# Two-layer decoder trunk, one core: ScalarE copies both halves of the transposed attention probabilities, and the end norm is applied to token rows

## The reference, cut to what matters

```python
# sliding window attention: 16 query heads of 64, 128-token blocks, window of 2 blocks
logits = jnp.concatenate([scores, sink], axis=-1)
m = jnp.max(logits, axis=-1, keepdims=True)
p = jnp.exp(logits - m)
probs = p[..., :-1] / jnp.sum(p, axis=-1, keepdims=True)
out = jnp.einsum('bkgnij,bnjkd->bnikgd', probs.astype(v.dtype), v2)
...
# after the two layers
y = x * lax.rsqrt(jnp.mean(x * x, axis=-1, keepdims=True) + NORM_EPS)
return y * final_norm
```

## Time and profile before

| | |
|---|---|
| median of 3 runs | 2602.13 us |
| the profiled execution, own time | 2599.23 us |
| its span, first to last instruction | 2597.4 us |
| TensorE busy | 2502.4 us (96%) |
| VectorE busy | 1537.0 us (59%) |
| ScalarE busy | 869.8 us (33%) |
| the two stretches with the head groups | 500 to 740 us, 1766 to 1996 us |
| from the last unit to the end | 2577.5 to 2597.4 us |

### The profile page before, as it was taken

One profiled execution on the slowest core, in us unless ns is written; L12 is line 12 of the kernel. 1 busy time (PEld: TensorE's weight loads), 2 busy tenths in 40 slices (PEclk: granted clock), 3 DMA queues, 4 the chain that ended last, 5 costly groups with the idle time before them and its releaser, 6 DMA issues.

```text
span 2597.4 us, 35934 instructions
## 1 busy us (share of the span) xinstructions
PE 2502.4 (96%) x11581; PEld 2045.3 (79%) x11581; DVE 1537.0 (59%) x2345; ACT 869.8 (33%) x1320; POOL 212.9 (8%) x167
## 2 busy tenths in 40 slices
PE   5999999999999999999999999999999999999998
PEld 4788888777678878888878888887777888788886
DVE  6876778566644467633477767866665445633333
ACT  2331233545422243222332222344543223331222
POOL 5100003000000040000030000210000002200001
PEclk7999999999999999999999999999999999999999
DMA  6465664311123425523336656532111343233332
GB/s 222 125 199 166 194 183 132 122 56 50 57 68 96 129 88 170 159 85 96 110 91 194 188 177 195 160 122 60 54 57 49 99 128 97 85 100 95 95 111 66
DMA packets 494952, 307.19 MB, mean 118 GB/s; under 512 B 8904, under 2 KB 488472, under 8 KB 494232
## 3 DMA queue, kind: packets, MB, share of 16 engines
q1 hardware_dynamic: 427288, 239.10, 31.1%
q10 hardware_dynamic: 67584, 67.12, 8.1%
HBM read 299.89 MB, written 6.29 MB: 118 GB/s over the span
## 4 chain that ended last, share of the span: by engine, by line
PE 76%; DVE 13%; ACT 5%; issue 4%; POOL 1%; DVEq 0%; DMA 0%; ACTq 0%; SPq 0%; POOLq 0%
PE ps_proj L1468 23%; PE ps_proj L1469 23%; PE ps_proj L1470 23%; ACT sb_scratch L680 2%; DVE sb_w_lo L871 2%; DVE sb_small L1142 2%; DVE sb_scratch L1139 1%; PE ps_mid L1624 1%; PE ps_mid L1626 1%; PE ps_mid L1625 1%; DVE sb_scratch L1162 1%; PE ps_mid L1672 1%; POOL sb_scratch L461 1%; DVE sb_h_lo L938 1%; DVE sb_scratch L883 1%
## 5 line engine op out<-in xcount | busy, mean ns | idle before, releaser
L1468 PE MATMUL ps_proj<-sb_a_hi,sb_w_hi 128*128 128x512 f32 x1888 | 736.1, 390 | 3.0 <-DVE sb_w_lo L871 3.0
L1470 PE MATMUL ps_proj<-sb_a_hi,sb_w_lo 128*128 128x512 f32 x1888 | 734.7, 389 | 0.0
L1469 PE MATMUL ps_proj<-sb_a_lo,sb_w_hi 128*128 128x512 f32 x1888 | 734.5, 389 | 0.0
L533 ACT ACTIVATE sb_w_hi<-sb_raw 128x1024 fp32r<-128x1024 f32 (+1 forms) x388 | 431.0, 1111 | 872.6 <-PE ps_proj L1470 833.2
L871 DVE TENSOR_TENSOR sb_w_lo<-sb_raw,sb_w_hi 128x1024 fp32r<-128x1024 f32 (+1 forms) x388 | 503.4, 1297 | 310.9 <-ACT sb_w_hi L533 295.5
L1468 PE MATMUL ps_proj<-sb_h_hi,sb_w_hi 128*128 128x512 f32 x1280 | 511.9, 400 | 10.7 <-DVE sb_w_lo L871 6.3
L1469 PE MATMUL ps_proj<-sb_h_lo,sb_w_hi 128*128 128x512 f32 x1280 | 502.7, 393 | 0.0
L1470 PE MATMUL ps_proj<-sb_h_hi,sb_w_lo 128*128 128x512 f32 x1280 | 502.2, 392 | 0.0
L1468 PEld LDWEIGHTS ps_proj<-sb_a_hi,sb_w_hi 128*128 128x128 f32 x1888 | 354.4, 188 | 79.4 <-issue 3.0
L1470 PEld LDWEIGHTS ps_proj<-sb_a_hi,sb_w_lo 128*128 128x128 f32 x1888 | 354.4, 188 | 73.3
L1469 PEld LDWEIGHTS ps_proj<-sb_a_lo,sb_w_hi 128*128 128x128 f32 x1888 | 354.4, 188 | 73.0
(11 more groups left out here) (162 smaller groups left out, 1863.4 us busy)
## 6 DMA issues: line engine op xcount, KB each, us to landing
sb_raw<-in_ffn_w_up SPq DMA_DIRECT2D x176, 512.0 KB, 3.8
sb_scratch<-in_w_ada ACTq DMA_DIRECT2D x128, 512.0 KB, 4.2
sb_raw<-in_w_in SPq DMA_DIRECT2D x100, 512.0 KB, 3.8
sb_raw<-in_ffn_w_down SPq DMA_DIRECT2D x64, 704.0 KB, 4.5
sb_raw<-in_w_branch_swa SPq DMA_DIRECT2D x16, 512.0 KB, 3.6
sb_raw<-in_w_branch_ret SPq DMA_DIRECT2D x16, 512.0 KB, 3.6
sb_raw<-in_w_out SPq DMA_DIRECT2D x16, 512.0 KB, 3.6
sb_scratch<-in_w_ada SPq DMA_DIRECT2D x14, 512.0 KB, 7.4
```

The lines of the kernel that those rows point to most:

```text
L533: act.activation(Whi[s][:, 0:n], raw[s][:, 0:n], ACT.Copy).then_inc(hi_ready, 1)
L1468: pe.matmul(bank, Whi[s][:, w], hi, start=first, stop=False)
L1469: pe.matmul(bank, Whi[s][:, w], lo, start=False, stop=False)
L1470: return pe.matmul(bank, Wlo[s][:, w], hi, start=False, stop=last)
```

## The change

Two edits that have nothing to do with each other.

**Probabilities.** TensorE signals once after all 8 transposes, ScalarE copies both banks to SBUF in one instruction over 1024 columns, VectorE's `probs_out` is gone, and `swa_values` waits for ScalarE alone.

**End norm.** The final gain is multiplied into x by ScalarE tile by tile while the last units still run (`final_scale`, only in the last layer), behind the squares of the same tile. TensorE transposes the scaled but not yet normalised tiles into all eight PSUM banks: tiles 0 to 3 right behind the last unit into `pM`, then the sums of squares, then tiles 4 to 7 into `last_banks`. The blocks of one bank now belong to the same 128 tokens, so `rstd` is a number per partition: VectorE (features 0 to 511) and ScalarE (512 to 1023) multiply by it as they copy out, in 4 instructions each. Spreading `rstd`, VectorE's 8 products and ScalarE's 8 copies are gone. SyncE stores four pieces, one for each 128 tokens.

```diff
@@ last_banks @@
+        last_banks = [pA[0], pA[1], pO, pS]
@@ SyncE @@
-            for h in range(2):
-
-                sp.wait_ge(o_tok, 4 * (h + 1))
-                sp.dma_start(out[0].rearrange("(t p) d -> p t d", p=P)[:, :, 512 * h:512 * (h + 1)],
-                             out_tok[:, :, 512 * h:512 * (h + 1)]).then_inc(stored, 16)
-            sp.wait_ge(stored, 32)
+            for n in range(TT):
+
+                sp.wait_ge(o_first, n + 1)
+                sp.wait_ge(o_last, n + 1)
+                sp.dma_start(out[0].rearrange("(t p) d -> p t d", p=P)[:, n, :], out_tok[:, n, :]).then_inc(stored, 16)
+            sp.wait_ge(stored, 16 * TT)
@@ ScalarE @@
+            def final_scale(k):
+
+                act.activation(XV[:, k, :], XV[:, k, :], ACT.Copy, scale=vcols[:, bass.ds(GAIN_COL["final"] + k, 1)]).then_inc(z_ready, 1)
...
                                 square(3 * l + (3 if f else 1), 2 * j + s, s, bank_free[s], g0 + HALF + j + 2)
                                 in_next_layer(act, l, f, lambda: scaled_hi(3 * l + (3 if f else 1), 2 * j + s))
+                                if f:
+                                    in_last_layer(act, l, lambda: final_scale(2 * j + s))
...
             def probs_out(no):
-                act.wait_ge(pt_ps, 2 * no + 1)
-                act.activation(probs_t[:, 0:T], pM[:, 2, :], ACT.Copy).then_inc(pt_act, 1)
+                act.wait_ge(pt_ps, no + 1)
+                act.activation(probs_t.rearrange("p (a t) -> p a t", a=2), pM[:, 2:4, :], ACT.Copy).then_inc(pt_act, 1)
...
-            for k in range(KT):
-                act.wait_ge(y_out, k + 1)
-                act.activation(out_tok[:, :, P * k:P * (k + 1)], pA[k % 2][:, :].rearrange("p (t c) -> p t c", c=P),
-                               ACT.Copy).then_inc(o_tok, 1)
+            act.wait_ge(rstd_ready, 4 * DEPTH + 1)
+            for n in range(TT):
+                act.wait_ge(y_last, n + 1)
+                act.activation(out_tok[:, n, T:2 * T], last_banks[n][:, :], ACT.Copy, scale=rstd[:, n:n + 1]).then_inc(o_last, 1)
@@ VectorE @@
-            def probs_out(no):
-                dve.wait_ge(pt_ps, 2 * no + 2)
-                dve.tensor_copy(probs_t[:, T:2 * T], pM[:, 3, :]).then_inc(pt_dve, 1)
...
                     retention_rope(1, rk)
-                    probs_out(h0)
                     maxima(h0 + 2, l, i, 1, 0, 0)
                     normalise(h0 + 2, 0)
                     retention_gate(0)
-                    probs_out(h0 + 1)
                     maxima(h0 + 3, l, i, 1, 1, 1)
...
                     swa_out(2 * n0, 2 * i)
-                    probs_out(h0 + 2)
...
-                    probs_out(h0 + 3)
...
-            dve.wait_ge(rb_ready, 4 * DEPTH + 1)
-            for k in range(KT):
-                if k >= 2:
-                    dve.wait_ge(y_out, k - 1)
-                g = vcols[:, GAIN_COL["final"] + k:GAIN_COL["final"] + k + 1]
-                dve.scalar_tensor_tensor(tbuf[k % 2], pO[:, :], g, XV[:, k, :], ALU.mult, ALU.mult).then_inc(t_ready, 1)
+            dve.wait_ge(rstd_ready, 4 * DEPTH + 1)
+            for n in range(TT):
+                dve.wait_ge(y_first, n + 1)
+                dve.tensor_scalar(out_tok[:, n, 0:T], pM[:, n, :], rstd[:, n:n + 1], None, ALU.mult).then_inc(o_first, 1)
@@ TensorE @@
                         last = pe.transpose(pM[:, 2 + a, P * n:P * (n + 1)], probs[w][:, T * a + P * n:T * a + P * (n + 1)], ident)
-                    last.then_inc(pt_ps, 1)
+                last.then_inc(pt_ps, 1)
...
                 pe.wait_ge(pt_act, no + 1)
-                pe.wait_ge(pt_dve, no + 1)
...
+            def turn(bank, n, k, first):
+
+                return pe.transpose(bank[:, P * (k - first):P * (k - first + 1)], XV[:, k, P * n:P * (n + 1)], ident)
+
+            half = KT // 2
+            for k in range(half):
+                pe.wait_ge(z_ready, k + 1)
+                for n in range(TT):
+                    last = turn(pM[:, n, :], n, k, 0)
+                    if k == half - 1:
+                        last.then_inc(y_first, 1)
             sum_squares(3 * DEPTH)
-            spread_rstd(4 * DEPTH, pO, 0).then_inc(rb_ready, 1)
-            for k in range(KT):
-                pe.wait_ge(t_ready, LAYER_SPLITS * DEPTH + k + 1)
-                if k >= 2:
-                    pe.wait_ge(o_tok, k - 1)
-                for t in range(TT):
-                    last = pe.transpose(pA[k % 2][:, P * t:P * (t + 1)], tbuf[k % 2][:, P * t:P * (t + 1)], ident)
-                last.then_inc(y_out, 1)
+            for s in range(2):
+                pe.wait_ge(bank_free[s], LAYER_GATED * DEPTH + 1)
+            for n in range(TT):
+                if n == TT - 1:
+
+                    pe.wait_ge(rstd_ready, 4 * DEPTH + 1)
+                for k in range(half, KT):
+                    pe.wait_ge(z_ready, k + 1)
+                    last = turn(last_banks[n], n, k, half)
+                last.then_inc(y_last, 1)
```

More of the change, by code:

```diff
@@ L224, in decoder @@
         scores, max_ready, exp_ready, p_ready = sem("scores"), sem("max_ready"), sem("exp_ready"), sem("p_ready")
-        pt_ps, pt_act, pt_dve, o_ps, o_hi, o_done = (sem(n) for n in ("pt_ps", "pt_act", "pt_dve", "o_ps", "o_hi", "o_done"))
+        pt_ps, pt_act, o_ps, o_hi, o_done = (sem(n) for n in ("pt_ps", "pt_act", "o_ps", "o_hi", "o_done"))
         st_ps, st_done, y_ps, ysq, ysum, y_free, var_ps = (sem(n) for n in ("st_ps", "st_done", "y_ps", "ysq", "ysum", "y_free", "var_ps"))
         mg_ready, mg_hi, mg_lo = sem("mg_ready"), sem("mg_hi"), sem("mg_lo")
-        y_out, o_tok, stored = sem("y_out"), sem("o_tok"), sem("stored")
+        z_ready, y_first, y_last, o_first, o_last, stored = (sem(n) for n in ("z_ready", "y_first", "y_last", "o_first", "o_last", "stored"))
         carrier = {"pool": sem("pool_carrier"), "dve": sem("dve_carrier")}
@@ L314, in in_next_layer, with in_last_layer @@
                     work()
+        def in_last_layer(eng, l, work):
+            with eng.If(l > DEPTH - 2):
+                work()
         def next_layer(l):
```

## The result

The changed kernel took 2585.43 us as the median of 4 runs (2583.16 to 2586.3); the kernel before 2601.85 beside it (4 runs, 2599.65 to 2603.2). The profiled execution took 2585.38, its span 2583.6.

The account below looks back on a forecast made before the run. TensorE, busy 96% of the span, was taken as the bound, so only its idle time and the end could be won: 7.6 + 5.9 = 13.5 us off 2602.1 gives 2588.6 us, range 2586 to 2593.

Parts of the forecast that it names:

- the short waits in the head groups: TensorE's waits for VectorE's copy and maxima in 8 head groups: 7.6 us to be won in all.
- Values of h0: Head groups: the 0.70 us wait for VectorE's copy goes, 0.10 returns at scores of h0+3; net 0.60 each.
- Retention scores: Head groups: earlier maxima of h0+3 close the 0.14 us gap ahead of these scores; 0.12 counted each.
- Values of h0+2: Head groups: earlier maxima let ScalarE's copy end before TensorE comes, so the 0.32 us wait goes in each.
- Last step of head group 3: Transposes to values, no unit between: the longer ScalarE copy makes 0.88 us idle 1.24, a loss of 0.36, twice.
- cross-check with the 10.7 us of the waits' view: Head groups: summing from TensorE's 10.7 us of waits for VectorE's copy gave a gain of 7.7 us.
- No new wait: Head groups: waits for ScalarE's copy, about 1.2 us, only in head group 3; maxima waits up some 1.5.
- The end: Behind the last product: first store 5.6 us sooner, four stores' data without a gap; 5.9 us won.
- stores that pay their fixed part one by one: Rival at the final stores: each pays its fixed 1.43 us again; 4.3 us less won, 2592.9, chance 0.08.
- the rate of `x_spill`: Rival at the final stores: 2048 KB take 8.7 us from issue to landing; 1.8 less won, 2590.4, chance 0.17.
- The clock at the end: TensorE's clock around the final transposes: no cost counted; a fall would cost some 1.8 us, chance 0.02.
- carry to the median by the constant 2.9: Whole kernel: the runs' median stood 2.9 us above the profiled execution; that difference was carried over to the forecast.

Follow-up runs that it names:

- before again: The kernel before, nothing altered, run and profiled once more: 2603.21 us (one run).
- before filled: The kernel before plus 3 or 10 unused products between a norm's sum and the spreading of its factor: median 2597.96 us, ratio 0.9981.
- end norm alone: The changed kernel with the edit of the probabilities undone, so only the end edit against the kernel before: median 2595.82 us, ratio 0.9969.

## Why the prediction missed

The mechanism was right in each part, and two terms of the sum were too small, by more than the range allowed. The failed step is the pricing of the short waits in the head groups: 7.6 foreseen, 11.2 measured.

- **Values of h0**, 8 x 0.60 foreseen: 0.55 to 0.64 in head groups 0 to 2, 0.82 and 0.84 in head group 3, 5.2 in all. Right, but for head group 3, where a pause of 0.28 us in `normalise` of the step before (703.23 to 703.51, between the reciprocal and line 1162) is gone from VectorE's stream as well. It is a part of this edit's gain: all four traces with the old copies have it in both layers (before, before again, before filled, end norm alone), and none of the ten others has, the one with the copy of h0+1 put back included. What in VectorE's stream makes it is open.
- **Retention scores**, 8 x 0.12: 0.35 to 0.39 each, 3.0 in all where 0.96 was foreseen. This is more than half of the miss of 3.6. This step of the prediction read the gap between a modelled end and a start as the whole wait, and even took off from it; the copy put back alone costs 0.38 where 0.12 shows.
- **Values of h0+2**, 8 x 0.32: 0.38 to 0.41 each, 2.4 in the six of head groups 0 to 2, by the same fault.
- **Last step of head group 3**, a loss of 0.36: 0.25 by the rows above (the copy took 1.02, not 1.06). Together with values of h0+2 there it is a gain of 0.17 where 0.04 was to be lost.
- Sum of these by starts: 5.2 + 3.0 + 2.4 + 0.3 = 10.9; 0.3 stands elsewhere in the stretches. The period of a head group (scores of h0 to the next) fell by 1.34 to 1.39, 1.05 foreseen. The cross-check with the 10.7 us of the waits' view could not show the fault, since it sums the same gaps.
- **No new wait**: right. One for the long copy in head group 3 of each layer and nowhere else; maxima +1.7 (+1.5 foreseen); the retention products' 0.80 as it was.
- **The end**, 5.9: 6.4. `rstd` 0.80 late instead of 0.93, and 2 MB in 29 slices of 0.18, 5.2 us, instead of 5.5. The term took the 380 GB/s of rows of 2 KB; the new stores have rows of 4 KB and run at some 400. The rival, stores that pay their fixed part one by one, didn't come, and the rate of `x_spill` wasn't theirs either.
- **The clock at the end**: no cost, right. What was not thought of is that the clock elsewhere scatters by 2 to 4 us between two executions, so that one profile of each kernel compares luck as well: 13.8 here, 17.7 between two executions with the same pattern. The carry to the median by the constant 2.9 wasn't at fault for much: 2602.1 - 17.6 = 2584.5, and 2585.43 was measured.
- **The range** reached to 2586.0, 2.6 beyond the likeliest. It took what showed as the most that a short wait could cost. That each might cost up to a few tenths more than it shows was left without a price.

## What to carry to other kernels

Price a short wait on a pipelined engine from start to start, against the same pair where nothing holds it up; the idle time in the rows counts from a modelled end and held a third of the 0.38 us that one such wait cost (of 0.77 and 0.39 us at two others it held all but 0.07). Compare stretches cut at recorded starts, not two spans: here the layers of one and the same code repeat to 0.15 us in all but one trace (0.5 us), where whole executions scatter by 7. And where the engine that bounds the kernel pauses for a chain of small instructions, look at the clock behind the pause: products that nobody needs, put into it, gave 5.3 to 5.8 us.

## What the runs showed of the hardware

- ScalarE copies 128x1024 float32 out of two PSUM banks in 1.01 to 1.02 us, where two copies of 512 columns would take 2 x 0.58.
- One matmul group that has to wait at its head was slower behind it as well: the retention scores (two of 128x512 and two of 128x384), first start to the next group's start, took 1.31 after a wait of 0.12 and 1.21 without one. It is no rule: the values took 0.81 with a wait of 0.70 and without.
- Stores of 256 KB to 1 MB issued 0.4 to 1.3 us apart on one queue left no gap in their data. Where the second was issued 3.02 us after a first of 1 MB, some 0.8 us before the first one's data ended (kernel before), the rate fell to 33 GB/s in one slice of 0.185 us. Rows of 2 KB gave 384 to 386 GB/s and rows of 4 KB 399 to 408.
- Behind pauses of 1.6 to 3.4 us TensorE's granted clock fell to the lower level (1.2 GHz) in some executions and not in others, at the same place of the same program, and the dense matmuls went at 0.43 instead of 0.23 us for a while. During sixteen transposes in a row right behind dense work it was 1.00 (2569.8 to 2571.8 of the changed kernel).
